# Where the tiles of a one-core transformer kernel start in SBUF: moving tiles and weight buffers placed anew

## The reference

```python
# first_block (conditioned by c through w_ada)
proj = h @ w_in[l]                       # 1024 -> 3088, stick-breaking and gated linear attention
x = x + (1 + gate1) * (mixed @ w_out[l])
u = causal_depthwise_conv(h2 @ w_up[l], w_conv[l], b_conv[l])
x = x + (1 + gate2) * ((val * silu(gte)) @ w_down[l])
# second_block, layer A (RWKV) and layer B (MLA), each with
proj = h @ w_in;  x = x + concat(...) @ w_out
x = x + swiglu(rms_norm_2(x, g), w_gu, w_down)     # 1024 -> 2 x 2816 -> 1024
```

## The kernel before

| tile | before | after |
|---|---|---|
| raw0 to raw3 | 960 (0) | 0 (0) |
| whi0, whi1, whi2 | 960 (0) each | 32, 96, 160 (32) |
| wlo0, wlo1, wlo2 | 960 (0) each | 224, 288, 352 (32) |
| X, ub, rs_t, ssb, adac | 960 (0) | 352 (32) |
| h_hi, h_lo | 992 (32) | 512 (0) |
| m_hi, m_lo, kb_hi, kb_lo, c_hi, c_lo | 864 (32) | 256 (0) |
| mm_hi, mm_lo, mem_g | 896 (0) | 256 (0) |
| land (all of q1, k1, v1, gv, gg) | 864 (32) | 256 (0) |

## Time and profile before

### The profile page before, as it was taken

How to read it: one execution, slowest core, us unless ns; L and a number is a source line. 1 busy time by engine, 2 the same in 40 slices (tenths; PEclk the granted TensorE clock), 3 DMA queues, 4 the chain that set the end, 5 groups by cost and what they waited for, 6 DMA issues and landing times.

```text
span 1079.9 us, 22956 instructions
## 1 busy us (share of the span) xinstructions
PE 1043.6 (97%) x9990; PEld 989.0 (92%) x9990; DVE 734.0 (68%) x1194; ACT 562.2 (52%) x858; POOL 0.9 (0%) x7
## 2 busy tenths in 40 slices
PE   7999999999999999998899999999999999999997
PEld 6798898999999998887779999999989799999996
DVE  4798658899976667887547565566757665556554
ACT  4446374655655448754236444454667655444431
POOL 0000000000000000000000000000000000000000
PEclk8999999999999999999999999999999999999999
DMA  9958555466645553331004555356324435554451
GB/s 350 396 216 313 177 192 207 180 220 241 230 138 178 208 225 117 118 119 42 4 2 164 199 187 193 135 188 210 113 74 139 175 136 196 193 182 148 171 166 39
DMA packets 31236, 185.82 MB, mean 172 GB/s; under 512 B 3472, under 2 KB 4768, under 8 KB 13984
## 3 DMA queue, kind: packets, MB, share of 16 engines
q1 hardware_dynamic: 31136, 184.36, 47.8%
HBM read 183.29 MB, written 1.05 MB: 171 GB/s over the span
## 4 chain that ended last, share of the span: by engine, by line
PE 86%; DVE 6%; ACT 3%; DMA 2%; issue 2%; SPq 1%; DVEq 0%; ACTq 0%
PE banks L361 47%; PE banks L1361 17%; PE banks L341 4%; PE banks L358 2%; PE banks L637 2%; DMA land<-in_mkv_a 1%; DVE wlo L321 1%; PE banks L1904 1%; PE banks L1545 1%; ACT whi L306 1%; PE banks L1894 1%; PE banks L572 1%; DMA raw<-in_a_in 1%; DVE adac L556 1%; PE banks L640 1%
## 5 line engine op out<-in xcount | busy, mean ns | idle before, releaser
L321 DVE TENSOR_TENSOR wlo<-raw,whi 128x2048 fp32r<-128x2048 f32 (+3 forms) x163 | 323.1, 1983 | 174.4 <-ACT whi L306 173.8
L306 ACT ACTIVATE whi<-raw 128x2048 fp32r<-128x2048 f32 (+3 forms) x163 | 270.5, 1661 | 110.7 <-PE banks L1361 78.7
L361 PE MATMUL banks<-h_hi,whi 128*128 128x256 f32 x1376 | 180.6, 282 | 1.0 <-ACT h_hi L987 0.3
L361 PE MATMUL banks<-h_lo,whi 128*128 128x256 f32 x1376 | 179.6, 281 | 0.8 <-DVE h_lo L1062 0.8
L361 PE MATMUL banks<-h_hi,wlo 128*128 128x256 f32 x1376 | 177.7, 281 | 0.0
L361 PEld LDWEIGHTS banks<-h_hi,whi 128*128 128x128 f32 x1376 | 168.6, 188 | 4.7 <-ACT h_hi L987 2.1
L361 PEld LDWEIGHTS banks<-h_lo,whi 128*128 128x128 f32 x1376 | 167.7, 187 | 4.2 <-issue 2.6
L361 PEld LDWEIGHTS banks<-h_hi,wlo 128*128 128x128 f32 x1376 | 168.0, 188 | 1.6 <-issue 1.2
L1387 ACT ACTIVATE u<-u 128x256 f32<-128x256 f32 x44 | 18.4, 418 | 128.9 <-DVE u L1441 128.9
L1361 PE MATMUL banks<-m_lo,whi 128*128 128x256 f32 x528 | 75.6, 282 | 0.0
L1361 PE MATMUL banks<-m_hi,whi 128*128 128x256 f32 x528 | 75.5, 281 | 0.0
(11 more groups left out here) (449 smaller groups left out, 1405.8 us busy)
## 6 DMA issues: line engine op xcount, KB each, us to landing
raw<-in_ada SPq DMA_DIRECT2D x24, 1024.0 KB, 5.7
raw<-in_w_up SPq DMA_DIRECT2D x22, 1024.0 KB, 4.8
raw<-in_a_gu SPq DMA_DIRECT2D x22, 1024.0 KB, 4.8
raw<-in_b_gu SPq DMA_DIRECT2D x22, 1024.0 KB, 4.9
raw<-in_w_in SPq DMA_DIRECT2D x12, 1024.0 KB, 6.3
raw<-in_w_down SPq DMA_DIRECT2D x16, 704.0 KB, 4.1
raw<-in_a_in SPq DMA_DIRECT2D x11, 1024.0 KB, 5.0
raw<-in_a_down SPq DMA_DIRECT2D x16, 704.0 KB, 4.1
```

The lines of the kernel that those rows point to most:

```text
L306: act.activation(hi_s[k % NSPLIT][:, 0:w], raw[n % NRAW][:, 0:w], ACT.Copy).then_inc(*hi_made.tick(k))
L321: dve.tensor_tensor(lo_s[s][:, 0:w], raw[n % NRAW][:, 0:w], hi_s[s][:, 0:w].bitcast(F), SUB).then_inc(*lo_made.tick(k))
L361: i_ = pe.matmul(b[0:m, j * T:(j + 1) * T], a[:, kt * step + j * m:kt * step + j * m + m], x[:, kt, :], start=st, stop=sp)
```

## The change

Six fillers are laid before the split buffers, one before `raw`, one above `h_hi` on the right side and one before `S1`; `masks` and `one` change places, so that the 4 bytes of `one` no longer move what follows `masks`. The fillers are never read or written. No instruction is added, removed or moved, and no size or order of an operand is changed: the two programs differ in addresses alone.

```diff
         con = sb("con", [P, NCON])
+        sb("pad_low", [P, 16])
         raw = [sb(f"raw{i}", [P, SLOT]) for i in range(NRAW)]
-        hi_s = [sb(f"whi{i}", [P, SLOT], R) for i in range(NSPLIT)]
-        lo_s = [sb(f"wlo{i}", [P, SLOT], R) for i in range(NSPLIT)]
+        split = []
+        for i, n in enumerate((8, 16, 16, 16, 16, 16)):
+            if n:
+                sb(f"pad_w{i}", [P, n])
+            split.append(sb(f"whi{i}" if i < NSPLIT else f"wlo{i - NSPLIT}", [P, SLOT], R))
+        hi_s, lo_s = split[0:NSPLIT], split[NSPLIT:2 * NSPLIT]
         X = sb("X", [P, 8, T])
+        sb("pad_high", [P, 120], side="right")
...
+        masks = sb("masks", [P, 7, P], R)
         one = sb("one", [P, 1])
-        masks = sb("masks", [P, 7, P], R)
...
         gdec = sb("gdec", [P, 8], F, sc)
+        sb("pad_mix", [P, 248], F, sc)
         S1 = sb("S1", [P, 2, 4, 256], F, sc)
```

## The result

The changed kernel is slower: 1085.62 us as the median of 4 runs (1083.70 to 1087.43), against 1078.74 us before (4 runs). The ratio is 1.0066, with a 95% interval of 1.0049 to 1.0084. The profiled execution took 1086.29 us, its span is 1084.5 us, 4.6 us above that of before. The trace of before comes from an execution of 1081.68 us, 2.9 us above the median, so the two traces differ by less than the medians do. Each experiment's ratio is against executions of the kernel before that were taken alongside it. Medians, ranges and ratios are of fast runs alone: one execution of the last experiment, 1694.32 us at a granted clock of 0.556, is left out.

A forecast was written before the change was run, and what follows sets the result against it. TensorE's matmul interval was taken to bound the kernel; savings of 6.6 + 4.1 + 8.9 + 2.1 + 2.8 = 24.5 us took 1078.6 to 1054.1 us. The range was 1040 to 1088 us.

The forecast's parts named there:

- What bounds the kernel: Long TensorE stretches have no idle time, so only the interval between matmuls can carry a gain or loss.
- What that something may be: Moving tiles at multiples of 64 lie in 16 pieces, not 17, so their streams run at w_out's 113.4 ns.
- The size of the weight load has no part in it: Intervals with 64 or 16 stationary columns (116.9, 117.5 ns) are as with 128, so weight width doesn't matter.
- The sum: Matmul counts times interval savings: up products 6.6 + 4.1, down 8.9, others 2.1, rest 2.8; 24.5 us saved.
- Rival 1: Slower: weights 32 past a multiple of 64 cost more than aligned moving tiles return; 1086 to 1093 us, chance 0.28.
- the other products: Tile-ordered chunks, products after the attentions and w_out chunks; a 1.3 us loss if all ran at 118.8 ns.
- the rest: Some 1480 matmuls of w_in, a_in and layer B, woven into the attention parts; half counted, about 1 us lost.
- Rival 2: No effect: how streams fall into step, not the address, sets the interval; time stays 1078.6 us, chance 0.15.
- What should cost nothing: VectorE's time hardly depends on place; its share rises from 59% to 61%, so splits still come in time.
- the border that I had named: Borders of stages, the only places where a late split would cost time: the uncovered part of 2.3 us.

The follow-up runs named there:

- the last experiment: Kernel before with new distances and wlo2 as reset: wlo2 at 0, rest 64; at 128, rest 192; at 0, high 64, low 192: 1068.06, 1066.13, 1066.91 us.
- the run with 192: Kernel before with all moving tiles moved 64 bytes below the weights modulo 256 (distance 192, weights still at 960): 1068.25 us, ratio 0.991.

## Why the prediction was wrong, point by point

**What bounds the kernel: right.** The edit could act through the interval of the matmuls alone. The 4.6 us between the spans are the sum over TensorE's long stretches of the chain, VectorE's and ScalarE's groups kept their times (416 ns for m_lo, as in the earlier trace rows), and TensorE is busy for the whole of a stretch like that of the earlier trace rows, with 847 matmuls in 100 us instead of 860.

**The step that failed** is the reading of w_out in "What that something may be". I took the 113.4 ns of the earlier trace rows for a property of a moving tile at a multiple of 64, and counted pieces of 64 bytes. It is one of the two rhythms of distance 192. With everything at multiples of 64 the interval is 120.0 ns if the distance is 0, and shifting all by 32 bytes off that grid changed nothing. Two rows spoke against my reading and were there to be weighed: two of the three full chunks of w_out had 117.7 ns in the same places, and L358, whose moving operand also started at a multiple of 64, had 118.8 and 120.0 ns.

**"The size of the weight load has no part in it"** was wrong too, and it led to the step above: from "its width doesn't matter" I went on to look at the moving tile alone. The earlier trace rows compare streams at unlike distances. The row of 64 columns, 116.9 ns, is c at a distance of 160, where 128 columns have 118.7 or 120.0 ns; the 16-column tiles of w_gf start 64 bytes apart, so their rows mix four distances. At distance 0, 64 columns have 113.3 ns and 128 columns 120.0, as the run with all moving tiles at 960 shows. And the place of the weights matters as much as that of the moving tile, as the six intervals of the changed kernel show.

**The sum** multiplied the right counts by wrong differences. For the up products of f2 and f3 it had -3.3 ns for 2016 matmuls; measured are +1.75 ns. For their down products it had -5.3 ns, and got -0.2; for that of f1 -6.6, and got -1.3. So instead of -24.5 us came +6.9 us between the medians and +4.6 us between the traces.

**Rival 1** was the case that came true in sign and in size: it gave +7 us and 1086 us for 118.8 ns throughout, and the median is 1085.62 us. The measured time also lies inside the stated range. That the median agrees so closely is in part luck: between the traces it is +4.6 us, and of its terms the up products (5.6 us) measured 4.8, the other products (1.3 us) 0.6 in the two groups of 144, the down products -0.8 as against -0.6, and the rest, with 1 us in the sum, came to about nothing. Its mechanism, too, was only half right. It said that the changed kernel would run at the interval of the L358 rows, and it does, since those have the distances 224 and 96 that five of nine products now have. It gave as the reason that an operand lies 32 bytes off the grid of 64, and the run with all six buffers at 224, still 32 off, shows 116.7 ns and 1078 us. The chance of 0.28 was too low for the one combination that the trace had already measured.

**Rival 2** had a true part, the dependence on how a stream began. As a rival of its own it falls, since each buffer has its own interval and repeats it every three chunks.

**What should cost nothing** did so in the changed kernel. Of the faster versions it isn't true. I had argued from VectorE's share of 59% that the splits keep pace with chunks of 5.4 us. But VectorE and ScalarE wait for each other inside a chunk, and their round takes 5.58 us, at 59% busy; the share stayed at 58.9% in the run with 192 and didn't rise to 61%. So part of the forecast gain of the up products of f2 and f3 would not have come even at 113.4 ns. The loss shows as a wait of 0.86 us for `m_hi`, at the border that I had named.

**The Trainium skill beside the runs.** The measured intervals run from 113.3 to 120.0 ns at multiples of 32 bytes, and to 123.8 ns with the weights at a multiple of 16, with all shapes unchanged. The Trainium skill, SBUF — State Buffer, section "Door 1: The DMA port swizzle", with its lines of 16 bytes, would by itself have all of them equal, and the runs disagree. The Trainium skill, TensorE: Matmul & The Clock Gate, section "Step-by-step: what each phase is for", says that loading the next weights doesn't take read bandwidth from the running matmul, since each has a read port of its own. The measurement decides here: the place of the weights against that of the moving tile changes the interval by up to 6.7 ns, and so does its width at distance 0. What inside the memory causes it no run shows, and whether it is the two reads that meet is only argued.

## What to carry to other kernels

Where a TensorE stream has no idle time, compute the start of the stationary and of the moving operand modulo 256 and look at their difference before any alignment of the one or the other; with float32r operands and 128 stationary columns here a difference of 64 or 192 gave 113.3 ns in its good rhythm and 0 gave 120.0 ns, a spread of 6% on the 70% of the chain that L361, L1361, L341 and L358 make up. In this kernel 192 for all gained 0.9%, high buffers at 64 and low ones at 192 gained 1.5%, and 64 for all gained nothing that the runs could tell. Don't let buffers of a ring fall on whatever distances their fillers give. When the same instructions at the same places show two intervals in one trace, don't take the better one as the property of the place: ask what came before it. And before counting a gain on the engine that is always busy, follow the round of the other engines in the same stage: two that wait for each other can be at their limit at 59% and 44% busy.

## What the runs showed of the hardware

- The interval of a float32r matmul over 256 columns with 128 stationary columns goes with the difference of two SBUF addresses modulo 256: 113.33, 116.67, 117.8, 118.7 or 120.0 ns in steady stretches at one distance.
- A distance can have two steady rhythms, 113.33 and 117.8 ns at 64 and 192, 116.67 and 117.8 ns at 32, 118.7 and 120.0 ns at 160. A stage of over 1000 matmuls kept one from its start to its end, with VectorE, ScalarE and the DMA queues at work beside it.
- A short product in between (four matmuls of one column) can move the stream from one to the other, in both directions, and so can one product at another distance.
- 16 bytes can matter: distance 208 had 117.8 and 122.8 to 123.8 ns by turns (120.2 ns on the mean of f2's up product), between 113.3 or 117.8 ns at 192 and 118.1 to 118.8 ns at 224.
- The width of the weight load can matter: at distance 0 the interval was 113.3 ns with 64 stationary columns and 120.0 ns with 128.
